# A hybrid decoder block on one core: half of the first transposes move from TensorE to a trip through DRAM and VectorE

## The reference

```python
h = rmsnorm(x, g_mix[i])          # y = x * rsqrt(mean(x*x) + eps) * g
z = h @ w_in[i]                   # 1024 x 1536: a, b, v of 512 columns each
u = a * jax.nn.sigmoid(b)
u = causal_depthwise_conv(u, conv_w[i], conv_b[i])     # width 31
u = jax.nn.silu(layernorm(u, ln_g[i], ln_b[i]))
q = multiscale_pool(v, pool_w[i], pool_scale[i])
x = x + jnp.concatenate([u, q], axis=-1) @ w_out[i]
```

## Time and profile before

| | |
|---|---|
| runs | 1003.5 us median of 3 (1003.3 to 1003.97) |
| profiled execution | span 1001.1 us from the first to the last instruction |
| around the span | 1003.5 - 1001.1 = 2.4 us |
| TensorE busy | 990.6 us (99% of the span) |
| VectorE busy | 750.3 us (75%) |
| ScalarE busy | 464.0 us (46%) |
| GpSimd busy | 385.3 us (38%) |
| TensorE's granted clock | 0.999 of full speed |

### The profile page before, as it was taken

One profiled execution on the slowest core, in us unless ns is written; L12 is line 12 of the kernel. 1 busy time (PEld: TensorE's weight loads), 2 busy tenths in 40 slices (PEclk: granted clock), 3 DMA queues, 4 the chain that ended last, 5 costly groups with the idle time before them and its releaser, 6 DMA issues.

```text
span 1001.1 us, 12499 instructions
## 1 busy us (share of the span) xinstructions
PE 990.6 (99%) x4543; PEld 822.1 (82%) x4543; DVE 750.3 (75%) x1017; ACT 464.0 (46%) x713; POOL 385.3 (38%) x288
## 2 busy tenths in 40 slices
PE   9999999999999999999999999999999999999996
PEld 7888888888888888888888888888888888888885
DVE  6899999956699575665665665763687888985887
ACT  7635348414363423333333333333444665675775
POOL 3446797710146444444354354451000000011745
PEclk9999999999999999999999999999999999999999
DMA  7421202551224233333332332413998788533222
GB/s 255 152 71 43 85 1 120 205 178 64 105 64 132 80 105 111 100 106 95 116 105 83 127 105 70 141 64 107 359 388 301 232 310 261 196 106 105 85 84 105
DMA packets 103518, 138.25 MB, mean 138 GB/s; under 512 B 6122, under 2 KB 60930, under 8 KB 103458
## 3 DMA queue, kind: packets, MB, share of 16 engines
q1 hardware_dynamic: 103312, 137.20, 40.8%
q10 hardware_dynamic: 146, 0.27, 0.1%
HBM read 104.68 MB, written 32.77 MB: 137 GB/s over the span
## 4 chain that ended last, share of the span: by engine, by line
PE 95%; DVE 2%; issue 1%; ACT 1%; POOL 1%; DMA 0%; POOLq 0%; ACTq 0%; DVEq 0%
PE ps L1552 31%; PE ps L1554 31%; PE ps L1553 31%; PE ps L1606 2%; DVE ftmp L2414 0%; DVE resid L2417 0%; DMA resid<-in_x 0%; DVE spare L1958 0%; ACT junk L975 0%; PE ps L1700 0%; PE ps L1710 0%; ACT act_hi L961 0%; POOL rs L705 0%; PE ps L1690 0%; POOL ss L702 0%
## 5 line engine op out<-in xcount | busy, mean ns | idle before, releaser
L702 POOL TENSOR_SCALAR ss<-ss 128x1 f32<-128x1 f32 x38 | 16.8, 441 | 320.1 <-ACT junk L975 298.8
L2049 DVE SCALAR_TENSOR_TENSOR ps<-resid,convw,ps 128x512 f32<-128x512 f32 x190 | 127.4, 750 | 0.0
L1552 PE MATMUL ps<-ring_hi,ring_lo 128*128 128x512 f32 x308 | 120.0, 390 | 0.1
L1554 PE MATMUL ps<-ring_hi 128*128 128x512 f32 x308 | 119.8, 389 | 0.0
L1553 PE MATMUL ps<-ring_lo,ring_hi 128*128 128x512 f32 x308 | 119.8, 389 | 0.0
L1552 PE MATMUL ps<-act_hi,bs_lo 128*128 128x512 f32 x240 | 93.6, 390 | 0.0
L1554 PE MATMUL ps<-act_hi,bs_hi 128*128 128x512 f32 x240 | 93.4, 389 | 0.0
L1553 PE MATMUL ps<-act_lo,bs_hi 128*128 128x512 f32 x240 | 93.4, 389 | 0.0
L961 ACT ACTIVATE ring_hi<-raw 128x512 fp32r<-128x512 f32 x89 | 51.9, 625 | 60.4 <-PE ps L1554 60.3
L708 POOL TENSOR_TENSOR wc_lo<-raw_b,wc_hi 128x1024 fp32r<-128x1024 f32 x22 | 58.4, 2656 | 48.7 <-ACT wc_hi L961 47.6
L1958 DVE TENSOR_TENSOR ring_lo<-raw,ring_hi 128x512 fp32r<-128x512 f32 x89 | 58.0, 688 | 22.9 <-ACT ring_hi L961 22.7
(11 more groups left out here) (279 smaller groups left out, 2713.7 us busy)
## 6 DMA issues: line engine op xcount, KB each, us to landing
raw<-in_w_gate_up SPq DMA_DIRECT2D x44, 512.0 KB, 5.2
raw<-in_scratch SPq DMA_DIRECT2D x52, 256.0 KB, 3.3
raw<-in_w_down SPq DMA_DIRECT2D x52, 256.0 KB, 4.1
in_scratch<-in_s SPq DMA_DIRECT2D x44, 256.0 KB, 2.7
in_scratch<-gtmp SPq DMA_DIRECT2D x33, 256.0 KB, 2.3
keep<-in_w_down SPq DMA_DIRECT2D x32, 256.0 KB, 4.6
keep<-in_scratch SPq DMA_DIRECT2D x25, 256.0 KB, 3.5
resid<-in_x SPq DMA_DIRECT2D x8, 512.0 KB, 7.0
```

Of the source, the lines that this page charges most:

```text
L702: pool.tensor_scalar(ss[:, n:n + 1], ss[:, n:n + 1], 1.0 / D, EPS, ALU.mult, ALU.add)\
L1552: pe.matmul(dst, w_lo_, m_hi, start=start, stop=False, skip_group_check=onto)
L1554: return pe.matmul(dst, w_hi_, m_hi, start=False, stop=stop, skip_group_check=onto)
L2049: dve.scalar_tensor_tensor(out=conv_c if k == last_odd else acc, in0=u_all[:, c, k + h * BANK:k + (h + 1) * BANK], scalar=convw[:, c * 32 ...
```

## The change

- Tiles 4 to 7 are not transposed by TensorE. SyncE stores each normed tile (512 KB) into a new DRAM tensor `xt_scratch` and loads it back in four transfers, one for each group of 32 partitions, whose runs are 32 elements (128 bytes) long. The order of the runs is such that a transpose of every 32x32 block gives the transpose of the whole tile. The loads land in `wide`, two places in turn.
- VectorE transposes the blocks (`turn_x`), one instruction of 128x1024 for each tile, behind taps 1, 5, 9 and 13 of unit 0. Its eight `turned_lo` of these tiles are gone.
- ScalarE makes the high part in one instruction of 128x1024 per tile instead of two of 128x512 (`xt_high`), for tiles 4 and 5 ahead of `evac_ab(2)`, for 6 and 7 ahead of `evac_ab(3)`.
- GpSimd makes the low parts (`xt_low`), four instructions of 128x1024 behind `gate_u(2)`.
- The normed tiles 6 and 7 stand in `raw_b`. So SyncE loads p and `pool_w` only behind the last low part.
- TensorE waits for the four low parts (`xt_lo`) ahead of step n = 4. The transposes of the constants come in the middle of `first_part(1, back)`.
- In units 4 to 7 the work between taps stands 2 to 10 taps earlier than before (all four `q_low` 8 or 9).
- Some semaphores are merged (`gfin_in` into `gain_in`, three of the layer norm into `stats_ok`, four of `in_stored` into one), and counts of `turned` are shifted by a helper `turns`.

```diff
@@ SyncE
 def xn_place(n):
-            return scr[:, n % 2, :]
+            return raw_b[:, n % 2, :] if n in (6, 7) else scr[:, n % 2, :]
+        def xt_landing(t):
+            return wide[:, 1 + t % 2, HEADPAD:]
...
+            def store_xt(t):
+                sp.wait_ge(xn_ok, t + 1)
+                sp.dma_start(xt_dram[t], xn_place(t)).then_inc(xt_stored[t % 2], DMA)
+            def load_xt(t):
+                sp.wait_ge(xt_stored[t % 2], DMA * (t // 2 - 1))
+                if t >= HT + 2:
+                    sp.wait_ge(xt_turned, t - HT - 1)
+                for a in range(P // SQ):
+                    src = xt_dram[t].rearrange("(b j) (k a i) -> a j k b i", j=SQ, a=P // SQ, i=SQ)[a]
+                    sp.dma_start(xt_landing(t)[a * SQ:(a + 1) * SQ, :].rearrange("j (k b i) -> j k b i", k=KD, i=SQ), src)\
+                      .then_inc(xt_in[t % 2], DMA)
+            store_xt(4)
+            store_xt(5)
             sp.wait_ge(w_lo, S_B)
             load_cols(w_in_v, 256, C + 256)
+            load_xt(4)
+            load_xt(5)
+            store_xt(6)
+            store_xt(7)
+            load_xt(6)
+            load_xt(7)
+            sp.wait_ge(xt_lo, HT)
             sp.dma_start(raw_b[:, :, :].rearrange("p a (t d) -> p (a t) d", d=DP), p_v).then_inc(rawb_in, DMA)
@@ GpSimd
+            def xt_low(t):
+                pool.wait_ge(act_hi_ok, 2 * HT + t - HT + 1)
+                at = (slice(None), slice(None), slice(t * P, (t + 1) * P))
+                lo(act_lo[at], xn_place(t).rearrange("p (k s) -> p k s", k=KD), act_hi[at], xt_lo)
...
             gate_u(2)
+            for t in range(HT, TT):
+                xt_low(t)
             unit_begun(1)
             gate_u(3)
@@ ScalarE
+            def xt_high(t):
+                act.wait_ge(xt_turned, t - HT + 1)
+                copy(act_hi[:, :, t * P:(t + 1) * P], xn_place(t).rearrange("p (k s) -> p k s", k=KD), act_hi_ok)
...
-            turned_hi(4, 0)
-            turned_hi(5, 0)
             square_x(6)
             square_x(7)
             evac_ab(0)
             for m in range(2):
                 split_cols(m, 2 * DMA, bs_hi)
-            turned_hi(6, 0)
-            turned_hi(7, 0)
             first_taps(0)
             evac_ab(1)
             for m in range(2, 4):
                 split_cols(m, 2 * DMA, bs_hi)
             first_taps(1)
+            xt_high(4)
+            xt_high(5)
             evac_ab(2)
+            xt_high(6)
+            xt_high(7)
             evac_ab(3)
@@ TensorE
             first_part(0, back)
-            turn(4, 0)
-            turn(5, 0)
-
+            first_part(1, back, range(4))
             pe.wait_ge(const_in, 6 * DMA)
...
-            first_part(1, back).then_inc(ab_mm, 1)
+            first_part(1, back, range(4, KD)).then_inc(ab_mm, 1)
...
                 if n == KC:
-                    pe.wait_ge(act_lo_ok, 2 * TT)
+                    pe.wait_ge(xt_lo, HT)
                 ab_part(n, 0)
-                if n == 1:
-                    turn(6, 0)
-                    turn(7, 0)
@@ VectorE
-            turned_lo(4, 0)
-            turned_lo(5, 0)
             normed(6, 0, 1)
             normed(7, 0, 1)
...
-            turned_lo(6, 0)
-            turned_lo(7, 0)
-            dve.wait_ge(act_lo_ok, 2 * TT)
+            dve.wait_ge(act_lo_ok, 2 * HT)
...
+            def turn_x(t):
+                dve.wait_ge(xt_in[t % 2], P // SQ * DMA * (t // 2 - 1))
+                dve.transpose(xn_place(t), xt_landing(t)).then_inc(xt_turned, 1)
...
-            for j in range(KC):
+            convolve(0, {1: lambda: turn_x(4), 5: lambda: turn_x(5), 9: lambda: turn_x(6), 13: lambda: turn_x(7)})
+            for j in range(1, KC):
                 convolve(j, {})
-            convolve(4, {13: lambda: ln_stats(range(0, 2)), 19: lambda: ln_scale(range(0, 2)),
-                         25: lambda: ln_stats(range(2, 4))})
-            convolve(5, {3: lambda: ln_scale(range(2, 4)), 23: silu_0})
-            convolve(6, {2: mix_low_0, 9: silu_2, 11: mix_low_2, 17: lambda: q_low(0), 21: lambda: q_low(1),
-                         25: lambda: q_low(2)})
-            convolve(7, {3: lambda: q_low(3)})
+            convolve(4, {7: lambda: ln_stats(range(0, 2)), 13: lambda: ln_scale(range(0, 2)),
+                         18: lambda: ln_stats(range(2, 4))})
+            convolve(5, {1: lambda: ln_scale(range(2, 4)), 14: silu_0, 19: mix_low_0})
+            convolve(6, {2: silu_2, 4: mix_low_2, 9: lambda: q_low(0), 13: lambda: q_low(1),
+                         17: lambda: q_low(2), 21: lambda: q_low(3)})
+            convolve(7, {})
```

More of the change, by code:

```diff
@@ L35 @@
 HEADPAD = 16
+SQ = 32
 DMA = 16
@@ L187, in hybrid_block @@
         act_lo_ok = sem("act_lo_ok")
+        xt_stored = [sem(f"xt_stored{j}") for j in range(2)]
+        xt_in = [sem(f"xt_in{j}") for j in range(2)]
+        xt_turned = sem("xt_turned")
+        xt_lo = sem("xt_lo")
         w_hi = sem("w_hi")
@@ L267, in hybrid_block @@
         in_s_ok = sem("in_s_ok")
-        in_stored = [sem(f"in_stored{n}") for n in range(7)]
+        in_stored = [sem(f"in_stored{n}") for n in range(4)]
         ab_in = [sem(f"ab_in{j}") for j in range(6)]
@@ L646, in _ @@
                     if t == 0:
-                        for form in range(7):
+                        for form in range(3):
                             sp.wait_ge(in_stored[form], DMA * PAIRS)
+                        sp.wait_ge(in_stored[3], 4 * DMA * PAIRS)
                     sp.dma_start(xres[:, t, :], x1_dram[t]).then_inc(x_in[t], DMA)
@@ L831, in ln_rs @@
             def ln_rs(first, end):
-                pool.wait_ge(var_ok, end)
+                pool.wait_ge(stats_ok, 3 * end)
                 for t in range(first, end):
@@ L909, in times_post @@
                 if t == 0:
-                    pool.wait_ge(gfin_in, 2 * DMA)
+                    pool.wait_ge(gain_in, 4 * DMA)
                 e = e_place(t)
@@ L1200, in hi_b @@
                 elif q:
-                    act.wait_ge(turned, 2 * (TT + 7))
+                    act.wait_ge(turned, turns(TT + 7))
                 else:
@@ L1226, in hi_b22 @@
                 else:
-                    act.wait_ge(turned, 4 * TT)
+                    act.wait_ge(turned, turns(2 * TT))
                 copy(wc_hi[:, 2, :], b_block(q, 1, 1), wb22_hi)
@@ L1312, in gate_norm @@
                 if t >= 2:
-                    act.wait_ge(turned, 2 * n - 2)
+                    act.wait_ge(turned, turns(n - 1))
                 else:
@@ L1320, in even_high @@
                 for j in range(2):
-                    act.wait_ge(turned, 2 * n + j + 1)
+                    act.wait_ge(turned, turns(n) + j + 1)
                     if m:
@@ L1328, in a21_copy @@
             def a21_copy(m):
-                act.wait_ge(turned, 2 * (2 * TT + 2 * m + 1) + 1)
+                act.wait_ge(turned, turns(2 * TT + 2 * m + 1) + 1)
                 act.wait_ge(fs1_ok, FS + m)
@@ L1334, in odd_high @@
             def odd_high(m):
-                act.wait_ge(turned, 2 * (2 * TT + 2 * m + 1) + 2)
+                act.wait_ge(turned, turns(2 * TT + 2 * m + 1) + 2)
                 if m:
@@ L1519, in _ @@
             act.wait_ge(fs4_ok, FS + m + 1)
-            act.wait_ge(gfin_in, 2 * DMA)
+            act.wait_ge(gain_in, 4 * DMA)
             copy(pair(2), raw_b[:, 1, :], gain_ok)
@@ L2229, in in_forms @@
                 if j:
-                    for n in range(3, 7):
-                        dve.wait_ge(in_stored[n], DMA * j)
+                    dve.wait_ge(in_stored[3], 4 * DMA * j)
                 else:
@@ L2421, in final @@
                 if t == 0:
-                    dve.wait_ge(gfin_in, 2 * DMA)
+                    dve.wait_ge(gain_in, 4 * DMA)
                 x_ = x_tile(t, 3)[:, c]
```

39 lines of the change are left out of this document (20 added, 19 removed).

## The result

The changed kernel takes 1012.5 us (median of 4 runs, 1011.68 to 1014.22) against 1003.4 (1003.14 to 1003.97) on the same chip: a ratio of 1.0089, interval 1.0077 to 1.0101. The change costs 9.1 us; the forecast was a gain of 2, to 1001.5, with a range from 1000.2 to 1012.

A forecast was written before the change was run, and what follows sets the result against it. TensorE, busy 990.6 of 1001.1 us, was taken to bound the kernel. 1003.5 - 3.5 for its transposes + 1.45 for lateness at q_group(1) + 0.1 for restarting TensorE was given as 1001.5 us; 8-in-10 range 1000.2 to 1012.

The forecast's parts named there:

- Behind the start no other engine holds TensorE up; what is taken off its list shortens the kernel one for one: After the first 20 us, removing two blocks of sixteen TensorE transposes at 1.75 us each gains 3.5 us.
- The transposes on VectorE, 1.2 each: Four 128x1024 transposes in VectorE's unit 0 take 1.2 us each, 4.8 in all.
- Unit 0 starts 2.2 earlier: VectorE's first convolution unit begins at 35.9 instead of 38.11 us, as ScalarE's turned_hi work of 2.04 goes.
- S: VectorE's wait in unit 0 for the new transfers, taken as 0.8 us, for tile 6.
- the list of risks: Closing list of what else could be wrong, including SP held up in its queue so tiles 6 and 7 are stored late.
- the break-even point: Cost of a 128-byte run from which the change is a loss: 14.6 ns, where S = 2.85 us.
- gate_u(3) and sum_taps(2), which unit 2 needs some 17 us later; not late: GpSimd's work queued behind the four low parts, ending near 59.4 us, still comes in time for unit 2.
- the loss is the larger of 1.2 and 0.65 + S: TensorE's waits at step n = 4 (1.2 us) and q_group(1) (0.65 + S, 1.45 us) are not added.
- 1.2 us at step n = 4 for GpSimd's low parts: TensorE asks at 58.3 us, GpSimd's four low parts are signalled at 59.5: a wait of 1.2 us.
- 0.1 for starting TensorE again: Term of the sum for TensorE restarting after a wait, 0.1 us.
- Rival 1: Late transfers: 128-byte runs cost what 512-byte ones do, 24 to 28 ns; 1012.9 to 1017.3 us; chance 0.20 (above 17 ns).

## Why the prediction was wrong

- **"Behind the start no other engine holds TensorE up; what is taken off its list shortens the kernel one for one"** is the step that failed. No wait in the earlier trace rows means only that nobody was later than TensorE, not by how much everybody else was earlier. In the kernel before VectorE was ready 7.8 us ahead of the first conv_turn (118.06 - 110.23) and 3.2 ahead of the third (129.87 - 126.64), but only 1.0 ahead of the normed_turn that needs `mix_low(0)` (158.89 - 157.87) and 0.15 ahead of q_group(1). The last is a number that the prediction itself works out. Taking off 3.5 us gave 0.0; with 3.7 us off VectorE's list too, 3.5.
- **The transposes on VectorE, 1.2 each**: right, 1.24. Their price was not: the prediction set 4.8 us off against earlier places in the dictionaries (8 taps, 5.3 us). An earlier place makes one piece earlier and everything behind it later; the later taps and units are needed too. It can also come before its input: VectorE idled 4.1 us for ScalarE's `scale_shift` at the earlier places of `silu`, a wait that the prediction doesn't have. With the old places it was gone and the change was 0.0022 x 1003.5 = 2.2 us faster. The load of 5.0 us, put alone into the kernel before, cost 4.7.
- **"Unit 0 starts 2.2 earlier"**: nearly. 0.7 in the profiled execution, whose start was late among its like; over the profiled kernels 36.1 to 37.8 against 38.1 to 39.2.
- **S, VectorE's wait for the transfers, 0.8**: 4.1 (0.35 and 3.75). The packets of the changed kernel from 34 to 40 and from 44 to 52 us, nearly all of 128 bytes (packets, MB, share of 16 engines):

```profile
q1 hardware_dynamic: 5984, 0.76, 102.3%
```

```profile
q1 hardware_dynamic: 7473, 1.00, 79.2%
```

  A run cost 1.023 x 16 x 6.0 / 5984 = 16.4 ns and 0.792 x 16 x 8.0 / 7473 = 13.6 ns, not 12. The place was right, tile 6, and the rest of the lateness is SP, as the list of risks had it: it took 12.2 us to issue the eight loads of tiles 4 and 5, so that the stores left at 39.71 (tile 6 was normed by 28.4), landed 4.3 later instead of 2.6, and the load of tile 6 was waited for until 50.59 instead of 45.9. The 14.6 ns that the prediction gave as the break-even point was no such point: S = 2.85 was allowed for only because of the 3.5 us that weren't there.
- **"gate_u(3) and sum_taps(2), which unit 2 needs some 17 us later; not late"** and **"the loss is the larger of 1.2 and 0.65 + S"**: the loss isn't a maximum over TensorE's own next waits, since a late VectorE makes GpSimd wait (5.0 us ahead of the low parts of v), and TensorE behind that. So it came at v, where the prediction looked at nothing, and then at q_group(0) on top, since VectorE had lost more on the way (the 4.1 us at `silu`).
- **1.2 us at step n = 4 for GpSimd's low parts**: right, 1.16, in every version that kept their place.
- **"0.1 for starting TensorE again"**: 2.6 us of slower matmuls behind the wait at v, about 2.0 behind that at q_group(0).
- The Trainium skill ("DMA: Bandwidth & Descriptors", Specifications) with its penalty below 512 bytes was nearer to these transfers than the same page's three cycles on a packet (beside which the page has 32 bytes of descriptor for each): they moved 126 to 129 GB/s, against 290 to 345 with 512 bytes. Whether by a read-modify-write, no run shows. Rival 1 wasn't what happened: a run of 128 bytes took 13.6 to 16.4 ns, less than the 24 to 28 of one of 512. That the time came out just below rival 1's range is luck; the route was another.

Shown by the runs: the price of VectorE's load, of the short runs, that these act through VectorE's lateness, that the gain needs VectorE relieved, and what the earlier places cost in the changed kernel. Only read from the traces: what slowed the first taps beside GpSimd, and how the 3 us that remain with long runs divide between the low parts of GpSimd (1.2 at n = 4), VectorE's load and the places. Open: what the change is worth with the old places and early stores.

## What to carry to other kernels

An engine at 99% with no waits isn't the only bound: ahead of taking work off it, look at how late each other engine's result comes to it, at every place where it reads one, and take the smallest of these margins as the gain to expect (here 7.8, 3.2, 1.0 and 0.15 us: the gain was none). Busy shares by stretch say where to look; VectorE had 44.59 of 45 us here against 75% over the span. A wait in another engine's list that guards a buffer ties everything queued behind it to that event: follow lateness through these, and when you move such a wait, look at what its idle time protected: here two taps then ran beside GpSimd and took up to three times as long.

## What the runs showed of the hardware

- A load of 128 KB in 1024 runs of 128 bytes held SP for 12.16 / 8 = 1.5 us in the first eight and 6.80 / 8 = 0.85 in the second eight, so it isn't a fixed price; one in 32 runs of 4 KB held it for 4.39 / 8 = 0.55. Issues in SP's order of time (start, us), first of the change, then of the version with 4-KB runs:

```profile
27.51 12.16 SPq L577 DMA_DIRECT2D wide<-xt_scratch  x8
39.71 1.15 SPq L569 DMA_DIRECT2D xt_scratch<-raw_b  x2
44.00 6.80 SPq L577 DMA_DIRECT2D wide<-xt_scratch  x8
```

```profile
26.13 4.39 SPq L577 DMA_DIRECT2D wide<-xt_scratch  x8
30.57 0.90 SPq L569 DMA_DIRECT2D xt_scratch<-raw_b  x2
```

- A 32x32-block transpose of 128x1024 in float32 took 1.24 us on VectorE.
- Two VectorE taps with both operands in SBUF took 3.3 to 4.6 us beside a working GpSimd in four kernels, 1.42 with GpSimd waiting.
- Matmuls behind a wait followed at 0.43 us instead of 0.23, and not by the wait's length alone: some thirteen behind the 4.4 us at v; behind the same 2.4 us at q_group(0) some eight in the change and some six with 4-KB runs (granted clock 0.91 from 165 to 185 us in both), at most one in the version without transfers (1.00).
